# A three-layer fp32 forward pass on one core: step order changed at eleven places of the program

## Chip, core and metric

One NeuronCore of a Trainium2 chip runs the whole program in one launch. The metric is the device time of that core in microseconds (us); lower is better.

## What is computed

Batch 1, 256 tokens, width 1024, all in fp32. Three layers follow each other, and each ends in a feed-forward net with 2816 hidden channels:

```python
# layer 1: three branches of one projection, gated and summed, then w_out
y_a = mla_branch(u_mla, ...) @ w_br_mla       # softmax attention, 8 heads, low-rank q and kv, rope
y_b = fox_branch(u_fox, ...) @ w_br_fox       # softmax attention with a decay, 8 heads
y_c = ssm_branch(u_ssm, ...) @ w_br_ssm       # state-space scan, 16 heads, gated by z, normalised
merged = g[:, :, 0] * y_a + g[:, :, 1] * y_b + g[:, :, 2] * y_c
x = x + merged @ w_out
x = x + conv_ffn(rms_norm(x, norm_ffn_g), ffn_w_up, ffn_conv_w, ffn_conv_b, ffn_w_down)
# layer 2: causal mean pools and attention over 256 memory tokens, w_out, SwiGLU
# layer 3: stick-breaking attention (12 heads, keys and values from kv_norm(x) @ w_kv),
#          attention over the memory tokens (4 heads), w_out, SwiGLU
A[t, s] = sigmoid(z[t, s]) * prod(1 - sigmoid(z[t, j]) for j in range(s + 1, t))   # s < t
return rmsnorm(x, final_norm)
```

## The kernel before

**Layout.** Activations stay in SBUF with features on the partitions, as tiles [128, chunk, 256 tokens]; `x` is the residual stream with 8 chunks. Weights stream from HBM through a ring of four 1 MB slots (`ring`), one slot for 256 output columns.

**Products in three parts.** A dense group is 256 output columns. Its weights are split into a high part `w_hi` on ACT (line 1498, two halves) and the rest `w_lo` on DVE (line 1938, two halves); the activations are split too (`xhl`, `ssm_h`/`ssm_l`, `xn2h`/`xn2l`). TensorE (PE) sums high x high, high x low and low x high: 48 matmuls of 128x256 a group (line 949), or in the feed-forward layers 16 pairs of one matmul of 512 columns and one of 256 (lines 960, 961). There are two buffers of `w_hi`/`w_lo`, so the split of a group starts only when the group two before it has been multiplied. `split_before` and `SPLIT_AT` say at which group's step the split is issued; on ACT and DVE `splits(g)` stands ahead of the evacuation of group g. Groups go round four PSUM banks.

**Order.** `order()` writes one list `STEPS`, and each engine walks it and issues its own part of each step. `("g", stage, i)` is a dense group; `("half", stage, i)` issues only its first output half, and only on PE: ACT and DVE do nothing at it. The attention heads go in ticks (`ticks`, `first_layer`). At tick t: A, the scores of the pair (t, t+1) on PE; D, the product with the values of the pair before; C, the second PE step of head t-1 (transposes for softmax heads, suffix sums at lines 1358 to 1360 for stick-breaking heads, then DVE line 2298); B, the exponentials of head t (for a stick-breaking head four ACT operations of 128x384, lines 1722 to 1725, then DVE lines 2257, 2258); P, the division by the row sum; E, ACT line 1760; last comes what `fill(t)` gives, the dense groups of that tick. For the third layer the table `more` says which. There are three score banks (`stick_bank`: S0, S1 and T), so the scores of pair h, h+1 wait for DVE line 2298 of head h-2, and D waits for the E of both its heads.

**Output groups of the third layer.** `outb` takes no split: its four groups multiply raw fp32 weights with `mix_sb`, 16 matmuls each (lines 1009, 1043). `("ahead", i, m, k0)` issues a part of outb group i in an earlier tick: chunks 0 to 3 of output half m at k0 = 0 and chunks 4, 5 at k0 = 4; the group's own step then does chunks 6, 7.

**Norms.** `late(name, groups)` puts a norm behind the four quarters of a projection. For quarter i: DVE adds the group to `x` (line 2137), ACT writes the high part (line 1619), DVE the low part (line 2160), ACT the squares (line 1659), DVE adds them (line 2181). The first group of the next stage is multiplied in the order of the quarters, without the row factor; `total_sums` on PE (`"ns"`) follows, then Ln and Exp on ACT (lines 1681, 1690) give `rstd`, and DVE multiplies it in when it evacuates. Where the last group of a projection frees the buffer that the next split needs (`LAST_PAIR`), that split comes behind the squares of quarter 3: line 1668 on ACT, `behind` on DVE. Two small norms m6 and m7 of the first layer (keys of the MLA heads) stand in ticks 0 and 1 of the fox heads.

**Feed-forward nets.** `ffn(name)`: 22 up groups, each followed on ACT and DVE by the split for the group two later. In net "1" DVE scales the bank (line 2332) and does four convolution taps (line 2352), ACT applies SiLU (line 1818), and GpSimd (POOL) makes the hidden product and its two parts (lines 2502, 2504, 2506) for j = 0 to 19; for j = 20 and 21 DVE does these three (lines 2365, 2368, 2370).

**Ends.** PE begins with 11 matmuls of ones (line 1404) before the first weights are there. At the end DVE multiplies the four quarters of `x` with `rstd` (line 2210) and SyncE (SP) sends each to HBM (line 903).

Of the kernel before, what the change touches and what calls it, by code (L numbers as in the profile page):

```python
# [23 lines left out]
ALU = mybir.AluOpType  # L24
# [6 lines left out]
P = 128  # L31
# [227 lines left out]
def order():  # L259
# [69 lines left out]
    def first_layer(heads):  # L329
# [5 lines left out]
        for t in range(n + 2):  # L335
# [14 lines left out]
            out += {0: [("nm", "m6"), ("sq", "m7")], 1: [("nm", "m7")]}.get(t, [])  # L350
# [19 lines left out]
    st += [("g", "brs", 0), ("ns", "ssm", 3), ("nm", "ssm")] + [("g", "brs", n) for n in range(1, 4)]  # L370
# [155 lines left out]
def build(nc, cst_at, par_at, x_in, mem_in, pos_in, cst_in, cst2_in, par_in, w, out):  # L526
    with ExitStack() as ctx:
# [169 lines left out]
        tapped = sem("tapped")  # L697
        scaled, rest_copied = sem("scaled"), sem("rest_copied")
# [130 lines left out]
        def _(sp):  # L829
# [78 lines left out]
        def _(pe):  # L908
# [158 lines left out]
            def group(stage, i, half=None):  # L1067
# [81 lines left out]
                elif stage == "brs":  # L1149
                    last = feature3(stage, i, 256, two3, after("ssm") if i == 0 else None, (ssm_h, ssm_l))  # L1150
# [252 lines left out]
            for _ in range(11):  # L1403
# [69 lines left out]
        def _(act):  # L1473
# [18 lines left out]
            def high(raw, q, wait_landed, wait_used=None):  # L1492
# [4 lines left out]
                for a, e in halves_of(raw.shape[-1]):  # L1497
# [8 lines left out]
            def splits(g, behind=None):  # L1506
                for key in split_at(g, behind):
                    u, q = LOAD[key], SPLITS[key]
                    if q == 0:
                        continue  # L1510
                    high(ring[:, u % RING, 0:w[key[0]].shape[-1]], q, (landed[u % RING], 16 * (u // RING + 1)),
                         used(BY_SPLIT[q - 2]) if q >= 2 else None)
# [108 lines left out]

            def squares(name, i=None):
# [290 lines left out]
        def _(dve):  # L1913
# [20 lines left out]
            def low(raw, q, it, count):  # L1934

                for m, (a, e) in enumerate(halves_of(raw.shape[-1])):
                    dve.wait_ge(hi_ready, it * 2 * RING + (2 * count - 1 + m))
# [3 lines left out]
                last.then_inc(lo_ready, 1)  # L1941
# [605 lines left out]
```

## Time and profile before

| | |
|---|---|
| median of 3 runs | 1108.15 us (1107.95 to 1108.33) |
| the profiled execution | 1107.72 us; its span, first to last instruction: 1105.9 us |
| mean granted TensorE clock | 0.997 |
| busy | PE 98%, PE weight loads 89%, DVE 74%, ACT 57%, POOL 9% |
| PE instructions | 7444 matmul records |
| HBM traffic | 190.97 MB, 173 GB/s |

Busy time is the union of an engine's instructions from their start to their modelled end. Matmuls are pipelined: those of 256 columns start 0.118 us apart and each is shown for 0.28 us, so a wait appears some 0.17 us shorter than what it costs. The 16 matmuls of an outb group are recorded as 32 entries that start 0.2165 us apart; the scores of a pair of stick-breaking heads occupy PE for 0.85 us and the C of one for 0.89.

### The profile page before, as it was taken

How to read it: one execution, taken by the hardware profiler on the slowest of the kernel's cores; microseconds unless marked ns; L12 is line 12 of the kernel's file. 1: busy time of each engine (PE TensorE's matmuls, PEld its weight loads, DVE VectorE, ACT ScalarE, POOL GpSimd, SP SyncE). 2: the span in 40 equal slices, each digit the busy share in tenths (PEclk: the TensorE clock that was granted, in tenths of full speed). 3: DMA queues.
4: the chain of work that ended last, by engine and by line, in shares of the span. 5: the costliest groups of instructions: out<-in, count | busy, mean ns of one | idle time of the engine just before them, and what ended most of it. 6: DMA issues, size and time to landing. Idle time of an engine off the chain costs nothing.

```text
span 1105.9 us, 19448 instructions
## 1 busy us (share of the span) xinstructions
PE 1080.5 (98%) x7444; PEld 980.5 (89%) x7444; DVE 815.1 (74%) x1332; ACT 632.8 (57%) x1046; POOL 98.7 (9%) x112
## 2 busy tenths in 40 slices
PE   8999999999999999999999999999999999999997
PEld 8986999999999999988979888888899778888886
DVE  6856898668777999956765888876756447888654
ACT  6675767556657666644335655545567545555453
POOL 0000211056200333300000000000000000000000
PEclk9999999999999999999999999999999999999999
DMA  9345533455545556456426555445643036554451
GB/s 355 142 165 187 209 136 107 173 192 198 183 161 190 177 180 233 154 182 221 162 77 228 177 191 191 165 158 183 233 149 136 17 117 231 188 191 166 166 189 47
DMA packets 33899, 190.97 MB, mean 173 GB/s; under 512 B 3916, under 2 KB 7268, under 8 KB 16676
## 3 DMA queue, kind: packets, MB, share of 16 engines
q1 hardware_dynamic: 33252, 188.95, 48.4%
q10 hardware_dynamic: 576, 1.05, 0.3%
q8 instruction: 48, 0.79, 0.3%
q14 instruction: 23, 0.19, 0.0%
HBM read 187.86 MB, written 2.12 MB: 172 GB/s over the span
## 4 chain that ended last, share of the span: by engine, by line
PE 70%; DVE 16%; ACT 7%; issue 5%; DMA 1%; DVEq 1%; SPq 0%; ACTq 0%
PE bank L949 26%; PE bank L960 14%; PE bank L961 7%; DVE w_lo L1938 7%; DVE acc L2352 3%; PE S L960 3%; PE bank L1009 3%; ACT w_hi L1498 2%; PE O L960 2%; PE T L960 2%; PE S L961 2%; PE bank L1018 1%; PE O L1394 1%; PE O L961 1%; DVE pr L2332 1%
## 5 line engine op out<-in xcount | busy, mean ns | idle before, releaser
L1938 DVE TENSOR_TENSOR w_lo<-ring,w_hi 128x1024 fp32r<-128x1024 f32 (+2 forms) x354 | 379.3, 1113 | 97.9 <-ACT w_hi L1498 96.7
L1498 ACT ACTIVATE w_hi<-ring 128x1024 fp32r<-128x1024 f32 (+2 forms) x354 | 322.6, 961 | 192.7 <-PE bank L949 125.2
L949 PE MATMUL bank<-xhl,w_hi 128*128 128x256 f32 x1792 | 321.0, 282 | 1.9 <-DVE w_lo L1938 1.5
L949 PEld LDWEIGHTS bank<-xhl,w_hi 128*128 128x128 f32 x1792 | 273.4, 188 | 6.3 <-issue 4.9
L949 PE MATMUL bank<-xhl,w_lo 128*128 128x256 f32 x896 | 250.3, 279 | 0.0
L960 PE MATMUL bank<-hid,w_hi 128*128 128x512 f32 x528 | 184.9, 394 | 3.3 <-DVE w_lo L1938 2.9
L949 PEld LDWEIGHTS bank<-xhl,w_lo 128*128 128x128 f32 x896 | 168.8, 188 | 0.0
L961 PE MATMUL bank<-hid,w_lo 128*128 128x256 f32 x528 | 147.8, 280 | 0.0
L960 PE MATMUL bank<-xhl,w_hi 128*128 128x512 f32 x352 | 124.9, 392 | 1.3 <-DVE w_lo L1938 1.2
L960 PEld LDWEIGHTS bank<-hid,w_hi 128*128 128x128 f32 x528 | 99.2, 188 | 28.5 <-issue 6.0
L961 PE MATMUL bank<-xhl,w_lo 128*128 128x256 f32 x352 | 99.3, 282 | 0.0
L961 PEld LDWEIGHTS bank<-hid,w_lo 128*128 128x128 f32 x528 | 99.2, 188 | 0.0
L960 PEld LDWEIGHTS bank<-xhl,w_hi 128*128 128x128 f32 x352 | 66.1, 188 | 15.7 <-DVE w_lo L1938 2.0
L1793 ACT ACTIVATE pr<-bank 128x256 f32<-128x256 f32 x44 | 16.9, 385 | 106.4 <-PE S L961 52.2
L961 PEld LDWEIGHTS bank<-xhl,w_lo 128*128 128x128 f32 x352 | 66.7, 190 | 0.1
L2352 DVE SCALAR_TENSOR_TENSOR acc<-pr,par,acc 128x255 f32<-128x255 f32 (+1 forms) x88 | 56.4, 680 | 3.0 <-DVE acc L2352 0.2
L960 PE MATMUL S<-xhl,w_hi 128*128 128x512 f32 x160 | 56.3, 390 | 0.0
L961 PE MATMUL S<-xhl,w_lo 128*128 128x256 f32 x160 | 45.2, 282 | 0.0
L1619 ACT ACTIVATE xhl<-x,cst,par 128x256 fp32r<-128x256 f32 x40 | 21.8, 593 | 32.3 <-DVE x L2137 25.1
L2339 DVE TENSOR_TENSOR acc<-bank,pr 128x256 f32<-128x256 f32 x44 | 18.7, 425 | 26.8 <-ACT pr L1793 26.8
L960 PEld LDWEIGHTS S<-xhl,w_hi 128*128 128x128 f32 x160 | 30.0, 188 | 6.2
L960 PE MATMUL T<-xhl,w_hi 128*128 128x512 f32 x96 | 34.1, 390 | 0.0
(354 smaller groups left out, 1941.1 us busy)
## 6 DMA issues: line engine op xcount, KB each, us to landing
ring<-w_up SPq DMA_DIRECT2D x22, 1024.0 KB, 4.8
ring<-w_upa SPq DMA_DIRECT2D x22, 1024.0 KB, 4.8
ring<-w_upb SPq DMA_DIRECT2D x22, 1024.0 KB, 4.8
ring<-w_gate SPq DMA_DIRECT2D x12, 1024.0 KB, 4.9
ring<-w_down SPq DMA_DIRECT2D x16, 704.0 KB, 4.0
ring<-w_downa SPq DMA_DIRECT2D x16, 704.0 KB, 4.1
ring<-w_downb SPq DMA_DIRECT2D x16, 704.0 KB, 4.2
ring<-w_xbc SPq DMA_DIRECT2D x6, 1024.0 KB, 5.0
```

The costliest lines, as they stand in the source:

```text
L949: last = mm(out, lhs, rhs, start=(start and k == 0 and (a, b) == (0, 0)), **kw, stop=(whole and k == ks[-1] and (a, b) == (1, 0)))
L960: mm(both, w_of(0, k), x2_of(k), start=k == 0, stop=False, skip_group_check=True)
L961: last = mm(main, w_of(1, k), x2_of(k)[:, 0, :], start=False, stop=whole and k == ks[-1], skip_group_check=True)
L1009: last = mm(b[p0:p0 + width, m * S:m * S + S], W[0:kp, k * wide + c0:k * wide + c0 + width], src(k), start=(k == 0), stop=(k == kc - 1))
L1018: last = mm(b[:, tt * wide:(tt + 1) * wide], src(k)[:, tt * P:(tt + 1) * P], W[:, k * wide:(k + 1) * wide], start=(k == 0), stop=(k == kc ...
L1394: mm(outs[m][:, 0:S], vs[m][:, 0, :], probs[m][:, 0:S], start=True, stop=False)
L1498: A(w_hi[:, q % 2, a:e], raw[:, a:e], ACT.Copy).then_inc(hi_ready, 1)
L1619: last = A(hi[:, c, :], src[:, c, :], ACT.Identity, bias=C("zero"), scale=Pm(gain, c))
L1793: last = A(pr[:, r, m * S:(m + 1) * S], b[:, S:2 * S], ACT.Copy)
L1938: last = V.tensor_tensor(w_lo[:, q % 2, a:e], raw[:, a:e], w_hi[:, q % 2, a:e], ALU.subtract)
L2339: last = V.tensor_tensor(y[:, m * S:(m + 1) * S], b[:, 0:S], pr[:, r, m * S:(m + 1) * S], ALU.add)
L2352: ins = stt(part, y[:, m * S:(m + 1) * S - late], par[:, bass.ds(j * 8 + o, 1)], part, ALU.mult, ALU.add)
```

## The change

Seven kinds of edit. (1) The norm steps `nm m6`, `sq m7` and `nm m7` stand one tick later. (2) The first half of `brs 1` is issued on PE between `brs 0` and the sums of the norm "ssm". (3) `more` gives the dense groups of the stick-breaking ticks out anew. (4) Three outb groups are begun ahead instead of two, and the first two in one tick each. (5) For "ffn1" and "ffna" the split behind quarter 3 is cut in two: its first half stands ahead of the high and low part of quarter 3, the second where the whole stood. (6) In net "1" the hidden product of j = 20 goes to POOL. (7) PE begins with 17 matmuls of ones; at the end POOL multiplies quarter 2, and the quarters are sent in the order 0, 1, 3, 2.

```diff
@@ order(), first_layer
-            out += {0: [("nm", "m6"), ("sq", "m7")], 1: [("nm", "m7")]}.get(t, [])
+            out += {1: [("nm", "m6"), ("sq", "m7")], 2: [("nm", "m7")]}.get(t, [])
...
-    st += [("g", "brs", 0), ("ns", "ssm", 3), ("nm", "ssm")] + [("g", "brs", n) for n in range(1, 4)]
+    st += [("g", "brs", 0), ("half", "brs", 1), ("ns", "ssm", 3), ("nm", "ssm")] + [("g", "brs", n) for n in range(1, 4)]
...
-    more = [sum(both("kk", 1), []), *both("qq", 1), both("kv", 1)[0], both("kv", 1)[1] + both("kk", 2)[0],
-            both("kk", 2)[1] + both("qq", 2)[0], both("qq", 2)[1], *both("kv", 2), *both("qmb", 0)]
-    more += [[("ahead", i, m, 0)] for i in range(2) for m in range(2)]
-    more += [[("ahead", i, m, 4) for m in range(2)] for i in range(2)] + [[]]
+    more = [sum(both("kk", 1), []), sum(both("qq", 1), []), *both("kv", 1), *both("kk", 2), sum(both("qq", 2), []),
+            *both("kv", 2), *both("qmb", 0)]
+    more += [[("ahead", i, m, 0) for m in range(2)] for i in range(2)] + [[("ahead", 2, m, 0)] for m in range(2)]
+    more += [[("ahead", i, m, 4) for m in range(2)] for i in range(3)]
@@ SyncE
-            for i in range(4):
-                sp.wait_ge(normed, NORMED["last"] + i + 1)
+            for n, i in enumerate((0, 1, 3, 2)):
+                sp.wait_ge(*((pool_normed, 1) if i == 2 else (normed, NORMED["last"] + n + 1)))
@@ TensorE
-            for _ in range(11):
+            for _ in range(17):
@@ ACT, squares(name, i)
                 for wait in input_ready(name, i) if (name, i) != ("last", 3) else ():
                     act.wait_ge(*wait)
+                if name in ("ffn1", "ffna") and i == 3:
+                    split_behind(name, 0)
                 if name in LATE and name not in ("x1", "ssm"):
                     high_parts(name, i, 0)
...
                 if i == 3:
                     n["wide"] += 1
-                    for g, norm in LAST_PAIR.items():
-                        if norm == name:
-                            splits(g, behind=True)
+                    split_behind(name, 1 if name in ("ffn1", "ffna") else None)
@@ DVE, step "sq"
+                    early = s[1] in ("ffn1", "ffna")
+                    if early and s[2] == 3:
+                        behind(s[1], 0)
                     if s[1] not in ("x1", "ssm"):
                         low_parts(*s[1:], 0)
                     add_squares(*s[1:])
                     if s[2] == 3:
-                        behind(s[1])
+                        behind(s[1], 1 if early else None)
@@ DVE, end of ffn("1")
-                    dve.wait_ge(up_hid, NFF // RING * RING)
-                    for j in range(NFF // RING * RING, NFF):
-                        hidden(j, j % RING, j // RING)
+                    dve.wait_ge(hid_t, NFF - 1)
+                    dve.wait_ge(hid_high, NFF - 1)
+                    dve.wait_ge(up_hid, NFF - 1)
+                    hidden(NFF - 1, (NFF - 1) % RING, (NFF - 1) // RING)
@@ GpSimd
+                if s == ("nm", "last"):
+                    pool.wait_ge(gained, 3)
+                    pool.wait_ge(rstd_ready, len(NORM_AT))
+                    Q.tensor_tensor(x[:, 4:6, :], x[:, 4:6, :], rstd[:, 0:S].unsqueeze(1).to_broadcast([P, 2, S]), ALU.mult)\
+                        .then_inc(pool_normed, 1)
...
+                    up(NFF - 2, 0, NFF // RING, base)
```

Three places show what the order of the instructions becomes. In this list x3 is the number of equal instructions, and a line number is that of the kernel it is from.

ACT, third layer, ticks 3 to 5: `v_sb` is the evacuation of kv group 1, the operations on `sc` and `G` are the B of heads 4 and 5, `pT` is an E. Before:

```order
L1722 ACTIVATE sc<-S,cst 128x384
L1723 ACTIVATE sc<-S,cst 128x384
L1724 ACTIVATE sc<-sc,cst 128x384
L1725 ACTIVATE sc<-sc,cst 128x384
L1760 ACTIVATE pT<-pr,cst 128x384
L1498 ACTIVATE w_hi<-ring 128x1024 x2
L1530 ACTIVATE v_sb<-bank,cst,rT 128x256 x2
L1768 ACTIVATE mix_sb<-O 128x256
```

and with the change:

```order
L1501 ACTIVATE w_hi<-ring 128x1024 x2
L1533 ACTIVATE v_sb<-bank,cst,rT 128x256 x2
L1731 ACTIVATE sc<-S,cst 128x384
L1732 ACTIVATE sc<-S,cst 128x384
L1733 ACTIVATE sc<-sc,cst 128x384
L1734 ACTIVATE sc<-sc,cst 128x384
L1769 ACTIVATE pT<-pr,cst 128x384
L1777 ACTIVATE mix_sb<-O 128x256
```

The split and the evacuation that followed B and E of the tick now stand ahead of them; `mix_sb` is the output of the D that waits for this E.

PE, third layer, ticks 11 to 13: L1043 (L1044 with the change) is work of `ahead`, `S<-mk,qm` the scores of memory heads 0, 1, `T<-pr` the C of head 11, `O<-pT,v_sb` the D of heads 10, 11. Before:

```order
L1043 MATMUL bank<-mix_sb,ring 128x256 x4
L1341 MATMUL S<-mk,qm 128x256 x2
L1343 MATMUL S<-mk,qm 128x256 x2
L1358 MATMUL T<-pr,cst 128x256
L1359 MATMUL T<-pr,cst 128x128
L1360 MATMUL T<-pr,cst 128x128
L1043 MATMUL bank<-mix_sb,ring 128x256 x4
L1394 MATMUL O<-pT,v_sb 64x256 x2
```

and with the change:

```order
L1044 MATMUL bank<-mix_sb,ring 128x256 x8
L1342 MATMUL S<-mk,qm 128x256 x2
L1344 MATMUL S<-mk,qm 128x256 x2
L1359 MATMUL T<-pr,cst 128x256
L1360 MATMUL T<-pr,cst 128x128
L1361 MATMUL T<-pr,cst 128x128
L1044 MATMUL bank<-mix_sb,ring 128x256 x8
L1395 MATMUL O<-pT,v_sb 64x256 x2
```

Eight matmuls of 256 columns stand where four did, ahead of the scores and between C and D.

DVE, end of the norm "ffn1" (quarter 3): `x<-bank` adds the last group, `xhl` is the low part, `lnv` adds the squares, `w_lo` is the split of up group 1. Before:

```order
L2137 SCALAR_TENSOR_TENSOR x<-bank,x 128x512
L2160 SCALAR_TENSOR_TENSOR xhl<-x,par,xhl 128x256 x2
L2181 TENSOR_TENSOR lnv<-lnv,sqr 128x512
L1938 TENSOR_TENSOR w_lo<-ring,w_hi 128x1024 x2
L2375 UNCONDITIONAL_BRANCH
```

and with the change:

```order
L2149 SCALAR_TENSOR_TENSOR x<-bank,x 128x512
L1949 TENSOR_TENSOR w_lo<-ring,w_hi 128x1024
L2172 SCALAR_TENSOR_TENSOR xhl<-x,par,xhl 128x256 x2
L2193 TENSOR_TENSOR lnv<-lnv,sqr 128x512
L1949 TENSOR_TENSOR w_lo<-ring,w_hi 128x1024
L2389 UNCONDITIONAL_BRANCH
```

One of the two halves of the split now stands between the addition and the low part of quarter 3.

## Rows read from the trace of the kernel before

**Rows 1.** The page, busy time of the engines.
```profile
PE 1080.5 (98%) x7444; PEld 980.5 (89%) x7444; DVE 815.1 (74%) x1332; ACT 632.8 (57%) x1046; POOL 98.7 (9%) x112
```
**Rows 2.** Waits of PE: us in total, times, longest.
```profile
PE bank L960 <- DVE w_lo L1938: 4.1, 9, 1.2
```
**Rows 3.** Timeline of PE, 109 to 124: start, us, instruction, [idle before <- releaser].
```profile
109.33 0.67 PE L1280 MATMUL S<-sqr,cst 96*128 96x512 f32 x1 [0.73 <-DVE sc L2268]
...
123.97 0.37 PE L949 MATMUL bank<-xhl,w_hi 128*128 128x256 f32 x1
```
**Rows 4.** Timeline of DVE, 124 to 125.
```profile
124.46 0.56 DVE L2268 SCALAR_TENSOR_TENSOR sc<-S,G 128x384 f32<-128x384 f32 x1
```
**Rows 5.** Timeline of PE and DVE, 297 to 309, the norm "ssm".
```profile
297.90 1.13 PE L930 MATMUL T<-lnv,cst 128*128 128x256 f32 x4 [1.08 <-DVE lnv L2181]
...
306.20 2.35 DVE L1938 TENSOR_TENSOR w_lo<-ring,w_hi 128x1024 fp32r<-128x1024 f32 x2
```
**Rows 6.** Timeline of DVE and PE at the end of the norm "ffn1".
```profile
341.73 0.88 DVE L2160 SCALAR_TENSOR_TENSOR xhl<-x,par,xhl 128x256 fp32r<-128x256 f32 x2 [1.16 <-ACT xhl L1619]
...
342.77 0.40 PE L949 MATMUL bank<-xhl,w_hi 128*128 128x256 f32 x2
...
345.71 0.39 PE L949 MATMUL bank<-xhl,w_hi 128*128 128x256 f32 x1 [0.50 <-DVE w_lo L1938]
```
**Rows 7.** Timeline of ACT: the high part of a split of 256 output columns.
```profile
835.58 2.02 ACT L1498 ACTIVATE w_hi<-ring 128x1024 fp32r<-128x1024 f32 x2 [1.39 <-PE bank L949]
```
**Rows 8.** Timeline of PE at the end of the norm "ffna".
```profile
610.91 0.50 PE L960 MATMUL bank<-xhl,w_hi 128*128 128x512 f32 x1 [1.24 <-DVE w_lo L1938]
```
**Rows 9.** Timeline of DVE and PE, 461 to 473, last hidden channels of net "1".
```profile
461.77 2.83 DVE L2352 SCALAR_TENSOR_TENSOR acc<-pr,par,acc 128x255 f32<-128x255 f32 x4
...
466.73 1.78 DVE L2352 SCALAR_TENSOR_TENSOR acc<-pr,par,acc 128x255 f32<-128x255 f32 x4
...
470.67 3.37 DVE L1938 TENSOR_TENSOR w_lo<-ring,w_hi 128x704 fp32r<-128x704 f32 x4
...
472.50 0.47 PE L960 MATMUL bank<-hid,w_hi 128*128 128x512 f32 x1 [1.08 <-DVE w_lo L1938]
```
**Rows 10.** Timeline of ACT, SiLU of j = 21.
```profile
468.54 0.51 ACT L1818 ACTIVATE sg<-acc,cst 128x256 f32<-128x256 f32 x1 [1.81 <-DVE acc L2352]
```
**Rows 11.** Timeline of PE and ACT in the stick-breaking ticks, 820 to 839.
```profile
820.60 0.48 PE L1325 MATMUL T<-qk_sb 64*128 64x256 f32 x1 [0.88 <-DVE pr L2298]
...
831.34 0.58 ACT L1722 ACTIVATE sc<-S,cst 128x384 f32<-128x384 f32 x1 [0.47 <-PE T L1327]
...
837.50 1.00 ACT L1530 ACTIVATE v_sb<-bank,cst,rT 128x256 f32<-128x256 f32 x2
```
**Rows 12.** Timeline of PE, 878 to 894, D of heads 10 and 11, outb 0.
```profile
878.83 0.65 PE L1394 MATMUL O<-pT,v_sb 128*64 128x256 f32 x4 [1.42 <-ACT pT L1760]
...
893.60 0.46 PE L1043 MATMUL bank<-mix_sb,ring 128*128 128x256 f32 x1 [0.60 <-ACT mix_sb L1768]
```
**Rows 13.** Timeline of DVE and PE, quarter 3 of the norm "ffnb".
```profile
911.14 0.69 DVE L2137 SCALAR_TENSOR_TENSOR x<-bank,x 128x512 f32<-128x512 f32 x1 [1.14 <-PE bank L1009]
913.00 0.88 DVE L2160 SCALAR_TENSOR_TENSOR xhl<-x,par,xhl 128x256 fp32r<-128x256 f32 x2 [1.16 <-ACT xhl L1619]
...
915.11 0.39 PE L960 MATMUL bank<-xhl,w_hi 128*128 128x512 f32 x1
```
**Rows 14.** Timeline of DVE, the last multiplications.
```profile
1100.20 2.50 DVE L2210 TENSOR_TENSOR x<-x,rstd 128x512 f32<-128x512 f32 x4 [2.44 <-ACT rstd L1690]
```
**Rows 15.** Timeline of POOL: one operation alone, then beside a split.
```profile
109.74 0.72 POOL L2490 TENSOR_TENSOR G<-merged,cst 128x256 f32<-128x256 f32 x1
...
125.58 1.82 POOL L2490 TENSOR_TENSOR G<-merged,cst 128x256 f32<-128x256 f32 x1
```
**Rows 16.** PE at the start: timeline, and busy us (and clock) by stretch.
```profile
15.43 0.38 PE L949 MATMUL bank<-xrh,w_hi 128*128 128x256 f32 x1 [0.45 <-DVE w_lo L1938]
7.70:11.00 3.30, 3.12 (x15) 2.82 (x14) 2.54 (x6) 3.30 (x8) 0.00 (x0) 0.50 1.06 433
```

More of the change, by code:

```diff
@@ L697, in build @@
         tapped = sem("tapped")
+        pool_normed = sem("pool_normed")
         scaled, rest_copied = sem("scaled"), sem("rest_copied")
@@ L1149, in group @@
                 elif stage == "brs":
-                    last = feature3(stage, i, 256, two3, after("ssm") if i == 0 else None, (ssm_h, ssm_l))
+                    last = feature3(stage, i, 256, two3, after("ssm") if i == 0 else None, (ssm_h, ssm_l), half)
                 elif stage == "out1":
@@ L1490, in got, with high @@
                 return banks[g % RING], evacuated[g % RING]
-            def high(raw, q, wait_landed, wait_used=None):
+            def high(raw, q, wait_landed, wait_used=None, half=None):
                 act.wait_ge(*wait_landed)
@@ L1496, in high @@
                     act.wait_ge(*wait_used)
-                for a, e in halves_of(raw.shape[-1]):
+                for m, (a, e) in enumerate(halves_of(raw.shape[-1])):
+                    if half not in (None, m):
+                        continue
                     A(w_hi[:, q % 2, a:e], raw[:, a:e], ACT.Copy).then_inc(hi_ready, 1)
@@ L1504, in head_high, with splits @@
                 A(w_hi[:, 0, a:e], ring[:, 0, a:e], ACT.Copy).then_inc(hi_ready if i % 2 else head_hi, 1)
-            def splits(g, behind=None):
+            def splits(g, behind=None, half=None):
                 for key in split_at(g, behind):
@@ L1511, in splits @@
                     high(ring[:, u % RING, 0:w[key[0]].shape[-1]], q, (landed[u % RING], 16 * (u // RING + 1)),
-                         used(BY_SPLIT[q - 2]) if q >= 2 else None)
+                         used(BY_SPLIT[q - 2]) if q >= 2 else None, half)
             def group(stage, i):
@@ L1620, in high_parts, with split_behind @@
                 last.then_inc(xh_ready, 1)
+            def split_behind(name, half):
+                for g, norm in LAST_PAIR.items():
+                    if norm == name:
+                        splits(g, True, half)
             def squares(name, i=None):
@@ L1932, in copied, with low @@
                 dve.wait_ge(evacuated[g % RING], g // RING + 1)
-            def low(raw, q, it, count):
+            def low(raw, q, it, count, half=None):
                 for m, (a, e) in enumerate(halves_of(raw.shape[-1])):
+                    if half not in (None, m):
+                        continue
                     dve.wait_ge(hi_ready, it * 2 * RING + (2 * count - 1 + m))
@@ L1940, in low @@
                         last.then_inc(head_low, 1)
-                last.then_inc(lo_ready, 1)
+                if half != 0:
+                    last.then_inc(lo_ready, 1)
             def head_rest(i):
@@ L1948, in head_rest, with splits @@
                     .then_inc(lo_ready if i == 3 else head_low, 1)
-            def splits(g, behind=None):
+            def splits(g, behind=None, half=None):
                 for key in split_at(g, behind):
@@ L1954, in splits @@
                         continue
-                    low(ring[:, u % RING, 0:w[key[0]].shape[-1]], q, 0, q + 1)
+                    low(ring[:, u % RING, 0:w[key[0]].shape[-1]], q, 0, q + 1, half)
             def pair(ap, i):
@@ L2162, in low_parts, with behind @@
                 last.then_inc(normed, 1)
-            def behind(name):
+            def behind(name, half):
                 for g, norm in LAST_PAIR.items():
                     if norm == name:
-                        splits(g, behind=True)
+                        splits(g, True, half)
             def add_squares(name, i):
```

2 lines of the change are left out of this document (added).

## The prediction

> **What bounds the kernel.** I read the busy line of the page first: PE is busy 1080.5 us of a span of 1105.9 [rows 1]. Another engine can matter only where PE waits for it. The waits of PE come next; their largest line is the low part of a weight split, 4.1 us in nine waits [rows 2]. All of them are short, and the change touches eleven or so. Since the matmuls stay (six small ones apart), the question is how many of those waits go and how many new ones the new order makes. So I read the timelines around each edited place, and compare when the result that PE needs would be ready with when PE would ask for it. A wait shown on PE costs some 0.17 more than is shown, because the matmul before it is drawn 0.28 long while the next could have started 0.118 after it. Times are of the profiled execution, 1107.72 us; the median is 0.43 higher, and differences go onto the median. About 0.2% (2.2 us) is what a measurement of this kernel tells from no change.
>
> **m6 and m7 a tick later.** The product for m6 waits 0.73 for the masked scores [rows 3]; with 0.17 and a little of the work behind it, 0.95 goes. In tick 2 the product of m7 then stands on PE right behind the C of fox head 1, where now a dense matmul starts at 123.97 [rows 3]. Its bank is freed by DVE at 124.46 + 0.56 = 125.02 [rows 4]. A wait of 1.05 comes: **+0.1** (bounds: no new wait, -0.95; DVE later by one operation, +0.7).
>
> **Half of brs 1 ahead of the sums.** It removes 1.08 + 0.17 = 1.25 at 297.90 [rows 5]. The half group is 24 x 0.118 = 2.83 of work, so the sums and `rstd` come 2.83 - 1.25 = 1.6 later. DVE's chain from the sums to the split of brs 3 starts 8.30 behind the sums [rows 5]; about 0.55 of that is idle and can go. The split would start at 306.20 + 1.6 - 0.55 = 307.2 and end 2.2 later, at 309.4. PE, 1.25 earlier than now, asks for it at about 308.8. So 0.55 comes back: **-0.7** (bounds -1.25 and 0).
>
> **ffn1 and ffna, the split cut in two.** At ffn1 DVE now writes the low part of quarter 3 at 341.73 to 342.61, PE takes it from 342.77, and after the sums it waits 0.50 for the split [rows 6]. With the change ACT and DVE do one half of the split first. On ACT one of 1024 columns takes half of 2.02 [rows 7], and the low part waits for ACT's high part [rows 6]: it is ready 1.0 later, at 343.65. PE waits 0.95 there. The split is then done earlier, but the sums end 0.95 later too, which eats the 0.67 saved: **+0.3** (bounds: -0.67, if the low part were hidden, and +0.8). At ffna PE waits 1.24 behind the sums [rows 8]. DVE's operations from the last addition to the end of the split are the same ones in another order, and PE's next product needs the last of them: **0.0** (bounds -1.4, if ACT's part was the limit, and +0.8).
>
> **Hidden product j = 20 on POOL.** The four taps take 2.83 while POOL makes a hidden product and 1.78 while it doesn't [rows 9]. Those of j = 21 are the 1.78 ones, and would now run beside POOL: +1.05. DVE saves one hidden product, half of the time from 468.51 to 470.67, 1.08 [rows 9]. But this product now covers ACT's SiLU of j = 21, 0.51 long and started by the last tap [rows 10]; without it DVE stands still for that. Sum 1.05 - 1.08 + 0.51 = **+0.5**, behind a wait of PE that is already 1.08 [rows 9] (bounds: taps undisturbed, -0.55; POOL ready late, +0.9).
>
> **Stick-breaking ticks.** The wait of 0.88 for line 2298 before the scores of heads 2, 3 goes (1.05) [rows 11], and about 0.8 of waits of 0.1 to 0.2 behind it and before the C of heads 3 and 7. Where a split and an evacuation now stand ahead of B and E on ACT, the D that needs this E is later. For kv 1: split 2.02, `v_sb` 1.00, four operations of B at 0.59 each, E 0.6, in all 6.0 behind the end of the group [rows 7, 11]. PE has only the scores (0.85), C (0.89) and half a group (2.83) to do, 4.6, so it waits 1.5 in that tick; the same sum gives 0.8 for kk 2 in the tick of D of heads 0, 1. **+0.5** (bounds: new waits absent, -1.9; both twice as long, +2.8).
>
> **Memory heads, three groups ahead.** D of heads 10, 11 waits 1.42 and outb 0 waits 0.60 [rows 12]; with 0.17 each and 0.3 at C of head 11 some 2.6 goes, of which 0.5 returns as shorter cover. The third group's 12 matmuls, 24 entries of 0.2165, are 5.2 of work moved ahead of outb 0, so its own part starts at 893.60 + 5.2 - 2.1 + 0.5 (the term before) = 897.2. From there the norm "ffnb" is a chain on ACT and DVE: from 893.60 to the low part of quarter 3 at 913.88 are 20.3, with 1.14 and 0.2 of idle that waits for PE [rows 12, 13]. At least 18.9 stay, so the low part is ready at 916.1. PE, with 5.2 less of work in between, would be at it 21.5 - 5.2 = 16.3 behind, at 913.5 [rows 12, 13]: a new wait of 2.6. Now it is there at 915.11, so both third-layer parts together give **+1.0**, of which this one has +0.5. The 5.2 us of matmuls moved ahead fill waits, and the chain behind them gives the time back (bounds: chain no limit, -2.1; +1.5 with its idle unchanged).
>
> **Ends.** The four last multiplications take 2.50, 0.62 each [rows 14]. With POOL on quarter 2, DVE is done 0.6 earlier. POOL's operation of 256 columns took 0.72 alone, and 1.82 beside a split [rows 15]; one of 512 is then between 1.3 and 3.2. It starts with quarter 0, and its transfer goes last. At 1.3 the last transfer leaves 0.6 earlier, at 3.2 it leaves 0.7 later: **+0.1**. The row of 1.82 is longer by about one DVE operation of the split. The Trainium skill (SBUF — State Buffer, "Who interferes with whom") says that a DVE instruction with two SBUF inputs contends with a GpSimd instruction that reads SBUF, and that the loser fully blocks. By that rule three DVE operations and POOL's stand in a row here, and this term is +0.7 instead of +0.1. The row agrees with the rule. The warm-up of 17 ones instead of 11 lies ahead of weights that come no sooner: the first full group waits for DVE's split at 15.43, whatever the clock was before [rows 16]: **0.0**.
>
> **Sum:** 0.1 - 0.7 + 0.3 + 0.0 + 0.5 + 0.5 + 0.5 + 0.1 + 0.0 = +1.3. That gives 1109.0 for an execution like the profiled one and **1109.5** on the median.
>
> **Rivals.** (a) All eleven waits go and none comes. They are 0.95, 1.25, 0.67, 1.4 (ffna), 1.25 (hidden product), 1.05 + 0.8, 2.6 and 0.6 at the end, in all 10.6, which gives 1097.6. For it: PE has no more work. Against it: four of them end on DVE and ACT chains that lose no operation. (b) The new waits are real but half as long. They are 1.05, 0.55, 0.95, 0.5 + 1.25 (hidden), 1.5 + 0.8 and 2.6, in all 9.2; half is 4.6, and 1109.5 - 4.6 gives 1104.9. This happens if ACT and DVE stand further ahead in the new order than my sums of rows let them. (c) **Slower, by the clock at the start.** Between 7.7 and 11.0 the granted clock was 0.50, that is 1.2 GHz, with 15 matmuls in 3.12 us, 0.208 each [rows 16]. Ahead of that PE had stood idle between the ones and the weights. If the longer warm-up shifts that stretch so that some 25 more matmuls of the first group run at the low level, 25 x (0.208 - 0.118) = 2.3 comes on top: 1111.8. It decides from the point where PE's first group is later than the split at 15.43. The Trainium skill (TensorE: Matmul & The Clock Gate, Part 1) says the gate goes by how busy PE has been recently; which side of it the six more ones fall no row of before shows. (d) **Slower, by ACT in the ticks.** If the splits that now stand ahead of B and E start later than the end of the group they wait for, the new waits of D are twice as long: 2.8 instead of 0.5 for the ticks, 1111.8. (e) The new order only renames what PE waits for: each wait that is removed comes back at the next step with its size, as at m7, where -0.95 meets +1.05. Then nothing changes: 1108.15.
>
> **Chances.** Forecast 0.50, with a range of its own of 1106 to 1111 (same 0.42, faster 0.03, slower 0.05); (a) 0.07; (b) 0.24, of it same 0.04; (c) 0.08; (d) 0.06; (e) 0.05. So faster 0.30, same 0.51, slower 0.19. The range leaves out (a), the lower part of (b) and a part of (c): 1103.8 to 1111.6.
>
> **What would show it.** Waits of PE shown at the product of m7 (about 0.9 for `sc`), at the low part of quarter 3 in ffn1 (0.8), at D of heads 0, 1 and 2, 3 (0.6 and 1.3 for `pT`) and in up group 0 of net "b" (2.4 for `xhl`) would prove the steps; the waits of 1.42 and 0.88 gone in any case. If the sum of PE's waits falls by over 4 us, the chains are shorter than I take them, and the forecast is wrong on the fast side; a stretch at clock 0.50 that reaches beyond 15.4 would prove (c).

## Result: 1113.21 us where 1109.5 was forecast, and the profile after

| | before | changed |
|---|---|---|
| median of 5 runs, us | 1108.15 | 1113.21 |
| lowest to highest | 1107.95 to 1108.33 | 1111.45 to 1115.08 |
| ratio | | 1.0043, 95% interval 1.0029 to 1.0058 |
| the profiled execution | 1107.72 | 1111.45 |
| mean granted TensorE clock of single executions | 0.997 (the profiled one) | 0.994 to 0.998 |

The change makes the kernel slower by 0.4%. Two things are to be explained. The profiled execution, one of the quickest of the changed kernel, is already 3.7 us above that of before. The five of it spread over 3.6 us, where the five of before agree within 0.4. (In the later batches, of 21 to 33 executions, before spreads by 1.2 to 2.4 itself, so some of that contrast is due to five being few.) The page of the changed kernel, busy line:

```profile
PE 1081.8 (97%) x7456; PEld 981.1 (88%) x7456; DVE 814.2 (73%) x1328; ACT 636.0 (57%) x1048; POOL 104.3 (9%) x116
```

Against [rows 1] PE has 12 records more (six ones) and 1.3 us more of busy time; ACT has 3.2 us more in two instructions more. Those two instructions are loads of function tables, 1.28 each; they are the first surprise, below. The waits of PE in the changed kernel (us, times, longest):

```profile
PE bank L961 <- DVE xhl L2172: 3.2, 2, 2.3
PE bank L961 <- DVE w_lo L1949: 3.1, 8, 1.1
PE T L1368 <- DVE pr L2303: 2.4, 3, 1.1
...
PE O L1395 <- ACT pT L1769: 1.1, 1, 1.1
...
PE S L1281 <- DVE sc L2282: 1.0, 1, 1.0
PE bank L950 <- DVE xhl L2172: 0.8, 1, 0.8
PE bank L961 <- DVE hid L2384: 0.6, 1, 0.6
```

The largest line of before, `w_lo` [rows 2], went from 4.1 to 3.1. In its place stand waits that before did not have: for the low part of a quarter (3.2 and 0.8), for the masked scores before the product of m7 (1.0, where before had 0.7 at the product for m6), and for a hidden product (0.6). Placed over each other, matmul by matmul, the two traces show the same work later by these amounts: +0.4 behind m7's product, +1.2 behind the C near 145, +0.7 behind `brs 3`, +1.0 behind ffn1, +1.7 at the last hidden product, +1.8 behind ffna, +2.35 at quarter 3 of ffnb, +2.75 at the last matmul, +3.7 at the end of the span. The largest steps are at places that I had priced at 0.1: m6/m7 and the end. The stops themselves, in time order (timeline of PE, changed kernel):

```profile
344.51 0.50 PE L950 MATMUL bank<-xhl,w_hi 128*128 128x256 f32 x2 [0.79 <-DVE xhl L2172]
...
610.53 0.50 PE L961 MATMUL bank<-xhl,w_hi 128*128 128x512 f32 x1 [0.94 <-DVE xhl L2172]
...
829.64 0.65 PE L1395 MATMUL O<-pT,v_sb 128*64 128x256 f32 x4 [0.56 <-issue]
...
840.36 0.65 PE L1395 MATMUL O<-pT,v_sb 128*64 128x256 f32 x4 [1.12 <-ACT pT L1769]
...
917.45 0.50 PE L961 MATMUL bank<-xhl,w_hi 128*128 128x512 f32 x1 [2.31 <-DVE xhl L2172]
```

Four of them are the stops that the prediction placed: 0.8 at ffn1, 0.6 and 1.3 at the two D, 2.4 at ffnb. For the D at 829.64 the profile names no releaser (`issue`), so that it waits for `pT` is not shown there. The fifth, 0.94 at 610.53 in ffna, stands ahead of the sums, where the prediction had no new wait; it takes the place of the 1.24 behind them [rows 8]. The start of the kernel does not matter: between 7.7 and 11.0 the granted clock was 0.50 in the profile of before [rows 16] and 1.00 in that of the changed kernel, and PE's wait for the split ends at 15.43 and at 15.40.

### The profile page after: what moved, and what is told of

Its sections match the earlier page's. It is cut to its first block, busy times and chain, and to the rows that moved or that the text cites. A ratio compares the mean times of both kernels' runs of the same rounds, so it can differ in the third digit from the quotient of the medians.

```text
span 1109.7 us, 19481 instructions
## 1 busy us (share of the span) xinstructions
PE 1081.8 (97%) x7456; PEld 981.1 (88%) x7456; DVE 814.2 (73%) x1328; ACT 636.0 (57%) x1048; POOL 104.3 (9%) x116
## 3 DMA queue, kind: packets, MB, share of 16 engines
HBM read 187.86 MB, written 2.12 MB: 171 GB/s over the span
## 4 chain that ended last, share of the span: by engine, by line
PE 69%; DVE 17%; ACT 7%; issue 6%; DVEq 1%; DMA 1%; SPq 0%; ACTq 0%
PE bank L950 26%; PE bank L961 14%; DVE w_lo L1949 7%; PE bank L962 7%; DVE acc L2366 4%; PE S L961 3%; ACT w_hi L1501 2%; PE O L961 2%; PE S L962 2%; PE T L961 2%; PE bank L1010 2%; PE bank L1044 1%; PE bank L1019 1%; PE O L1395 1%; PE O L962 1%
```

## The experiments

Sixteen kernels were run beside before, whose median in the four batches was 1108.10, 1108.07, 1107.98 and 1108.00, with 1.2, 1.4, 1.4 and 2.4 from its lowest to its highest. Kernels with one edit had 11 executions, the larger ones mostly 5. "Before plus one edit" is the kernel before with that part of the change's diff alone.

### The 17 ones, the end, the cut split

The first question was where the spread of 3.6 us comes from. Rival (c) had it at the start.

Before plus the 17 ones:
```diff
-            for _ in range(11):
+            for _ in range(17):
```


> The kernel before with 17 ones at the start instead of 11 and nothing else. Theory 1: the spread of the changed kernel (1111.45 to 1115.08, where before lies within 0.4) comes from the start, where in some executions the half clock lasts longer. Then this kernel spreads by some us too, with a median of 1109 to 1111, and an execution at the top shows 0.50 behind 15.4 us. Theory 2: the spread comes from the new order or from POOL at the end. Then this kernel gives 1108.15 within 0.3, and its executions agree within 0.5.

Measured: 1108.08 (1107.64 to 1108.52), ratio 0.9999 (0.9990 to 1.0008). The warm-up costs and gives nothing.

The changed kernel with 11 ones:
```diff
-            for _ in range(17):
+            for _ in range(11):
```


> The changed kernel with 11 ones again. Theory 1: its executions agree within 0.5 and the median is that of the undisturbed profiled execution, 1111.5. Theory 2: median 1113.2 and a spread of 3 us as with 17 ones.

Measured: 1111.91 (1111.51 to 1114.94), ratio 1.0043 (1.0029 to 1.0056). The spread of 3.4 stays. The slowest two executions had a mean clock of 0.993 and 0.995, the three quick ones 0.998. So a longer time goes with a lower mean clock, and 11 ones do not cure it: six ones more at the start are not the cause.

The same with the old end as well:
```diff
-                        if i == 2:
-                            continue
...
-            for n, i in enumerate((0, 1, 3, 2)):
-                sp.wait_ge(*((pool_normed, 1) if i == 2 else (normed, NORMED["last"] + n + 1)))
+            for i in range(4):
+                sp.wait_ge(normed, NORMED["last"] + i + 1)
```


> The changed kernel with 11 ones and with the old end (DVE multiplies all four quarters, sent 0, 1, 2, 3). The two profiles give the end 1.0 us, of it 0.46 on DVE: so 1.0 less than the kernel with 11 ones alone, 1110.5. If POOL at the end did not cost anything and the 1.0 were chance, both are the same within 0.3. If the spread comes from POOL at the end, it is gone here and not there.

Measured: 1112.31 (1111.19 to 1113.19), ratio 1.0038 (1.0025 to 1.0052). Inconclusive: a step of 1.0 can't be seen in five executions that spread by 2 to 3. A spread of 2.0 is left with the old end, so the end alone does not make it.

Before plus the split cut in two for ffn1 and ffna (in ACT and DVE):
```diff
+                    early = s[1] in ("ffn1", "ffna")
+                    if early and s[2] == 3:
+                        behind(s[1], 0)
                     if s[1] not in ("x1", "ssm"):
                         low_parts(*s[1:], 0)
                     add_squares(*s[1:])
                     if s[2] == 3:
-                        behind(s[1])
+                        behind(s[1], 1 if early else None)
```


> The kernel before with only the split behind quarter 3 cut in two, for ffn1 and ffna. Read from the changed kernel's trace: +0.3 at ffn1 and +0.1 at ffna, so 1108.5. My prediction had +0.3 and 0.0. A rival: the wait for the low part of quarter 3 costs in full, +1.0 and +1.2, 1110.4.

Measured: 1108.53 (1108.10 to 1108.89), ratio 1.0004 (0.9995 to 1.0013), +0.43. As forecast within 0.1: a wait behind the sums is exchanged for one ahead of them.

### The third layer and net 1, alone

Before plus the new ticks (`more`, first statement of the diff), before plus the three groups ahead (its last two), and both:

> The kernel before with only the new dense groups of the stick-breaking ticks; outb groups ahead as before. In the changed kernel's undisturbed trace this stretch gives +0.4: 1108.5. Theory A: the spread of the changed kernel (up to 3.6 above its lowest, at a mean clock of 0.994 instead of 0.998) comes from new stops of PE in these ticks, behind which the clock falls in some executions; then this kernel spreads by 2 us or more, median above 1109. Theory B: the spread comes from the memory heads and the norm ffnb; then it agrees within 1 us.

> The kernel before with only the three outb groups ahead. Undisturbed: +0.1 (my prediction +0.5), 1108.2 to 1108.6. Theory B: its executions spread by 2 us or more and the clock of some is 0.993 to 0.995, since the matmuls that stood before ffnb are gone and PE now stops for 2.3 there; median above 1109. Theory A: within 1 us.

> Both third-layer parts on the kernel before. Undisturbed +0.5: 1108.6, and with the spread, wherever in the third layer it arises, a median of 1109.5 to 1110.5. If neither this kernel nor the two others spreads, the cause is in the first layer or in net 1.

Measured: ticks 1108.31 (1108.10 to 1109.00), +0.24, ratio 1.0003 (0.9993 to 1.0012). Ahead 1109.66 (1108.26 to 1110.49), +1.59, ratio 1.0012 (1.0002 to 1.0021). Both 1109.58 (1108.31 to 1110.38), +1.51, ratio 1.0013 (1.0004 to 1.0022). Theory A falls and theory B stands: the ticks are harmless within what eleven executions tell. With three groups ahead seven of eleven executions lie at 1109.41 and above, and the four others between 1108.26 and 1108.84; the mean clock of the seven is 0.995 to 0.997, that of the four 0.998. The profiled execution of this kernel is one of the seven. Timeline of PE, first the stop, then what follows it:

```profile
912.77 0.28 PE L961 MATMUL T<-xhl,w_lo 128*128 128x256 f32 x1
915.36 0.50 PE L960 MATMUL bank<-xhl,w_hi 128*128 128x512 f32 x1 [2.31 <-DVE xhl L2160]
...
915.81 0.39 PE L960 MATMUL bank<-xhl,w_hi 128*128 128x512 f32 x1
...
916.16 0.39 PE L960 MATMUL T<-xhl,w_hi 128*128 128x512 f32 x1
...
918.52 0.63 PE L960 MATMUL bank<-xhl,w_hi 128*128 128x512 f32 x1
918.95 0.41 PE L961 MATMUL bank<-xhl,w_lo 128*128 128x256 f32 x1
919.16 0.63 PE L960 MATMUL bank<-xhl,w_hi 128*128 128x512 f32 x1
```

and the same trace by stretches (busy us of PE, PEld, DVE, ACT, POOL, each with its count; then granted clock, DMA share, GB/s):

```profile
912.80:915.30 2.50, 0.25 (x2) 0.00 (x0) 1.34 (x4) 1.70 (x3) 0.00 (x0) 1.00 1.01 413
915.30:916.50 1.20, 1.14 (x6) 1.01 (x7) 1.03 (x3) 0.00 (x0) 0.00 (x0) 1.00 0.84 335
916.50:918.20 1.70, 1.70 (x7) 1.42 (x6) 0.00 (x0) 0.08 (x1) 0.00 (x0) 0.54 0.95 381
918.20:920.00 1.80, 1.80 (x7) 1.51 (x7) 0.13 (x1) 1.71 (x5) 0.00 (x0) 0.50 0.16 68
```

In the profiled execution of the changed kernel, which has the same stop of 2.31 (ending at 917.45), the stretch as far behind it reads:

```profile
918.60:920.30 1.70, 1.70 (x11) 1.50 (x10) 0.00 (x0) 0.62 (x2) 0.00 (x0) 1.00 1.00 419
```

In the kernel with three groups ahead PE stands still for 2.31. The next matmuls run at full clock, and one microsecond later the granted clock is 0.54, that is the 1.2 GHz level for nearly the whole stretch, and 0.50 up to 920.0. Seven matmuls fall into 1.70 us there, eleven in the changed kernel, where the clock stayed at 1.00. A pair of a 512- and a 256-column matmul starts every 0.35 at first (915.81, 916.16) and every 0.64 then (918.52, 919.16). The lag behind the trace of before grows here from 0.25 to 1.94. Half speed from about 916.6 to 920.0 loses just that 1.7. So the stop costs about 0.3 where the clock holds and 1.7 more in this execution, where it falls. That the clock of the other six fell at the same place is inferred from their times: this is the only kept trace with a low clock in the middle of the program. The Trainium skill (TensorE: Matmul & The Clock Gate, Part 1) has the gate set by how busy PE has been recently; the trace agrees, with the clock at 1.00 during the stop and 0.54 after it.

Before plus the hidden product of j = 20 on POOL:
```diff
-                    dve.wait_ge(up_hid, NFF // RING * RING)
-                    for j in range(NFF // RING * RING, NFF):
-                        hidden(j, j % RING, j // RING)
+                    dve.wait_ge(up_hid, NFF - 1)
+                    hidden(NFF - 1, (NFF - 1) % RING, (NFF - 1) // RING)
...
+                    up(NFF - 2, 0, NFF // RING, base)
```


> The kernel before with the hidden product of j = 20 on POOL. The changed kernel's trace has +0.75 here, my prediction +0.5: 1108.9. A rival: POOL and DVE only swap the work and nothing is paid, 1108.15; or the product is the one at which the spread arises, above 1109.5.

Measured: 1108.89 (1108.46 to 1110.68), ratio 1.0010 (1.0001 to 1.0020), +0.82. Four of eleven are at 1109.88 and above, 1.4 or more over the lowest: perhaps a second place at which the clock falls. The profiled execution was not one of them, and before spreads by 1.4 in this batch itself, so this is read from a few times alone and is not shown. The timeline of DVE and then of PE in this kernel:

```profile
467.10 2.77 DVE L2352 SCALAR_TENSOR_TENSOR acc<-pr,par,acc 128x255 f32<-128x255 f32 x4
470.54 0.42 DVE L2365 TENSOR_TENSOR sg<-sg,acc 128x256 f32<-128x256 f32 x1 [0.68 <-ACT sg L1818]
...
471.67 3.36 DVE L1938 TENSOR_TENSOR w_lo<-ring,w_hi 128x704 fp32r<-128x704 f32 x4
```
```profile
471.81 0.50 PE L960 MATMUL bank<-hid,w_hi 128*128 128x512 f32 x1 [0.58 <-DVE hid L2370]
472.14 0.28 PE L961 MATMUL bank<-hid,w_lo 128*128 128x256 f32 x1
473.50 0.47 PE L960 MATMUL bank<-hid,w_hi 128*128 128x512 f32 x1 [1.08 <-DVE w_lo L1938]
```

The taps take 2.77 where they took 1.78 [rows 9], DVE then waits 0.68 for SiLU, and the split starts at 471.67 instead of 470.67. Of that 1.0, 0.37 was there already when the four taps began (467.10 instead of 466.73); from there to the split are 4.57 instead of 3.94, +0.63. Each of my three terms is in the rows. What I had not counted is that PE also needs this hidden product itself, 0.58 at 471.81, ahead of the wait for the split that keeps its 1.08. Two stops now stand within 2 us. At the second PE is later than in before by 1.0, of which 0.4 is older: the product's own price is 0.6, as forecast within 0.1, and the rest of the +0.82 is not explained by this trace.

### Filling the stops

If the stop makes the clock fall, work without a purpose in its place should cure it, in spite of being more work. Before plus three groups ahead, with nine matmuls of ones at quarter 3 of ffnb:
```diff
                     for k0 in range(0, KC, step):
+                        if name == "b" and step == 2 and k0 == 6:
+                            idle_ones(9)
```


> The kernel with three outb groups ahead and nothing else, plus nine matmuls of ones (about 2.0 us) issued on PE into a bank that nobody reads at the point where it stood still 2.3 before quarter 3 of ffnb. Theory (clock): the half clock that the last trace shows behind this stop, 916.5 to 919, comes from the stop; with the ones it does not come, all executions lie at 1108.3 within 0.4 and the clock at 0.998. Rival (order): the spread comes from something else in the new order, and the ones change nothing or cost their 2.0: median 1109.7 or more, spread 2.

Measured: 1108.38 (1107.88 to 1108.88), ratio 1.0003 (0.9994 to 1.0013). No execution is above 1108.88, where without the ones seven of eleven were at 1109.41 and above. Two limits: the kernels with the ones ran in later batches than those without, never side by side (before spreads no less in the later ones); and two of the eleven here have a mean clock of 0.995 at 1108.66 and 1108.88, so the mean over a whole execution does not tell where it was low. Its PE timeline (nine matmuls of ones are 18 entries):

```profile
912.71 2.17 PE L915 MATMUL O<-pT 128*128 128x128 f32 x18
915.19 0.50 PE L965 MATMUL bank<-xhl,w_hi 128*128 128x512 f32 x1 [0.30 <-DVE xhl L2167]
```

PE resumes at 915.19, as late as without the ones, and the wait shown is 0.30 instead of 2.31. The chain that sets this moment is DVE's.

The changed kernel with the ones at ffnb and three and five ones around the last hidden products of net 1:
```diff
+                    def hidden(k):
+                        if stage == "down1" and k == 21:
+                            idle_ones(3)
+                        return up_hid, base + k + 1
                     for half in range(2):
+                        if (stage, i, half) == ("down1", 1, 0):
+                            idle_ones(5)
```


> The changed kernel with the nine ones at ffnb and with three and five ones at the two stops of PE around the last hidden products of net 1. Theory (clock): median 1111.5, the changed kernel's lowest, and a spread under 1. If only one of the two places falls, a spread of 1.6 stays. Rival: 1113.2 and a spread of 3.6 as before.

Measured: 1111.73 (1111.41 to 1112.18), ratio 1.0035 (1.0022 to 1.0049). The spread falls from 3.6 to 0.8, less than the 1.6 that was expected if one place still fell. That fits falls at both places, but both were filled at once, in five executions, and no trace shows a fall in net 1: which of the two the ones cured is open. What remains, +3.75 on before, is the price of the new order. Against its own before the changed kernel had +5.06, so about 1.3 more is ascribed to the falls of the clock. This depends on the draw: with 11 ones instead of 17, which cost nothing, the median of five was only 3.8 above before. Of those ten executions five lie between 1111.45 and 1111.91, three are 1.7 to 2.2 above the middle of these, with mean clocks of 0.995 and 0.996, and two are 3.4 and 3.6 above it, with 0.993 and 0.994. Falls of 1.7 at one and at two places would give this.

### The moved norms and brs

Before plus m6 and m7 a tick later (the diff's first edit):

> The kernel before with only m6 and m7 a tick later. The changed kernel's trace gives +0.4 at the product of m7 and +0.8 more at the C of a fox head near 145, together +1.2: 1109.3. My prediction was +0.1: 1108.2.

Measured: 1109.24 (1108.84 to 1109.90), ratio 1.0012 (1.0003 to 1.0021), +1.26. The timeline of ACT and then of DVE in this kernel:

```profile
128.21 1.28 ACT L1681 ACT_TABLE_LOAD   x1
129.51 0.69 ACT L1681 ACTIVATE lnv<-S,cst 128x512 f32<-128x512 f32 x1
130.27 1.28 ACT L1690 ACT_TABLE_LOAD   x1
131.57 0.72 ACT L1690 ACTIVATE rstd<-lnv,cst 128x512 f32<-128x512 f32 x1
```
```profile
132.32 0.74 DVE L2195 SCALAR_TENSOR_TENSOR mqk<-mqk,par,rstd 64x512 f32<-64x512 f32 x1 [3.13 <-ACT rstd L1690]
```

In the kernel before, ACT had this order, and later, at 146, PE had no wait:

```profile
120.19 0.68 ACT L1681 ACTIVATE lnv<-S,cst 128x512 f32<-128x512 f32 x1
120.96 0.72 ACT L1690 ACTIVATE rstd<-lnv,cst 128x512 f32<-128x512 f32 x1
...
125.00 1.28 ACT L1576 ACT_TABLE_LOAD   x1
126.30 0.72 ACT L1576 ACTIVATE sg<-acc,cst 128x512 f32<-128x512 f32 x1
```

and with the norms moved PE has it:

```profile
146.06 0.33 PE L1367 MATMUL T<-cst,pr 128*128 128x128 f32 x1 [0.56 <-DVE pr L2289]
```

In tick 2 the convolution's SiLU (`sg`) has brought another function table onto ACT. The Ln and the Exp of m7 stood ahead of it and needed no load; now each needs one, 1.28 us. DVE stands still for 3.13 until `rstd` is there, 2.56 of it for the two loads, and its splits and the masked scores behind that are late until 146, where PE waits for a division by the row sum. The lag of PE behind the trace of before grows by 0.4 up to the product of m7, which is ahead of the loads, and by 0.8 from there to 146. At other norms the kernel itself asks for one table that holds both functions (`exp_and_ln`, six loads in all, and none at their Ln and Exp); nothing asks for it here, and no kernel was run in which it did. The Trainium skill (ScalarE: Activation LUTs, "What ACT_TABLE_LOAD costs") gives 1.28 for the load, which the rows show, and 1.38 more for a drain, which they don't: Ln starts 1.30 after its load does.

To see whether it is m7's place or m6's own move, before plus m7 alone in tick 2:
```diff
-            out += {0: [("nm", "m6"), ("sq", "m7")], 1: [("nm", "m7")]}.get(t, [])
+            out += {0: [("nm", "m6"), ("sq", "m7")], 2: [("nm", "m7")]}.get(t, [])
```


> The kernel before with only the norm of m7 in tick 2; m6 and the squares of m7 stay in tick 0, so the stop of 0.73 before m6 stays. Theory (table): the cost of the moved norms is that ACT has the table of the SiLU loaded in tick 2 and loads one for Ln and one for Exp, 1.28 each, while DVE waits 3.1 for rstd; then it is +1.2 plus the 0.95 that m6 no longer gives back, 1110.1. Rival (m6): the cost comes from m6 and its squares in tick 1; then it is +0.2 at most, 1108.2.

Measured: 1110.12 (1109.86 to 1111.06), ratio 1.0020 (1.0011 to 1.0029), +2.12. The theory had +2.15. Moving m6 gives 0.9 back, as my prediction said; m7's place costs 2.1. This tells m7 from m6; that the cost of m7's place is the two loads rests on the rows above.

Before plus the half group of brs 1 ahead of the sums:

> The kernel before with only the half group of brs 1 ahead of the sums. My prediction: -0.7, 1107.4. The changed kernel's trace: -0.5, 1107.6. Rival: the row factor comes later than PE wants it by the whole 1.25, 1108.1.

Measured: 1107.65 (1107.19 to 1108.65), -0.33, ratio 0.9998 (0.9989 to 1.0007): its interval holds no change, but the profile shows the parts. Of the 1.25, 0.78 comes back in PE's wait for the split of brs 3, as the prediction had it with 0.55:

```profile
309.94 0.35 PE L949 MATMUL bank<-ssm_h,w_hi 128*128 128x256 f32 x1 [0.61 <-DVE w_lo L1938]
```

### The end alone, the sum, and a better version

Before plus the new end:

> The kernel before with only the new end (POOL multiplies quarter 2, quarters sent 0, 1, 3, 2). My prediction: +0.1, with both ends of the bounds at -0.6 and +0.7. The changed kernel's profile against that of before has DVE's last multiplication 0.46 later and the last transfers 0.6 later still: +1.0, 1109.1. Without contention POOL would be done before DVE and the time falls: 1107.5.

Measured: 1108.99 (1108.55 to 1109.23), +0.99, ratio 1.0006 (0.9997 to 1.0015). DVE and POOL in this kernel:

```profile
1100.38 2.96 DVE L2213 TENSOR_TENSOR x<-x,rstd 128x512 f32<-128x512 f32 x3 [2.44 <-ACT rstd L1691]
```
```profile
1100.49 1.70 POOL L2515 TENSOR_TENSOR x<-x,rstd 128x512 f32<-128x512 f32 x1 [636.08 <-ACT rstd L1691]
```

Three multiplications take 2.96 where four took 2.50 [rows 14]. At 0.62 each they would be 1.9, so DVE loses 1.1 while POOL works for 1.70. The end is at 1103.34, 2.96 behind the first multiplication instead of 2.50: 0.46. Two transfers instead of one are then still to be sent, since quarter 2 goes last: from DVE's end to the span's end are 3.77 (1103.34 to 1107.11) instead of 3.24 (1102.70 to 1105.94), another 0.53. Together 0.99. POOL is done with quarter 2 at 1102.19, ahead of DVE's last; sending it before quarter 3 might save part of the 0.53, which was not tried.

What is left when m6/m7, the cut splits, the hidden product and the end are undone, with the nine ones at ffnb:

> What is left of the change without m6/m7, the cut splits, the hidden product and the end, and with the nine ones at ffnb: brs -0.4, ticks +0.2, three groups ahead +0.3, 17 ones 0: 1108.1. If the parts hinder each other, it is off by more than 0.4.

Measured: 1108.27 (1108.05 to 1109.13), ratio 1.0002 (0.9993 to 1.0011), +0.27. The same parts measured alone add up to -0.33 + 0.24 + 0.40 - 0.02 = +0.29.

The last kernel tries to take the chain at ffnb away instead of covering it. It has the half of brs 1 and the three groups ahead, and the split of up group 1 stands behind quarter 3 instead of in front of it:
```diff
+MOVED = [("upb", 1)]
+for _g in list(SPLIT_AT):
+    SPLIT_AT[_g] = [key for key in SPLIT_AT[_g] if key not in MOVED]
+SPLIT_AT.setdefault(GROUP["outb", 3], []).extend(MOVED)
...
-    late = [key for key in SPLIT_AT.get(g, []) if LAST[BY_SPLIT[SPLITS[key] - 2]] == g
-            and BY_SPLIT[SPLITS[key] - 2] not in HALVES] if g in LAST_PAIR else []
+    late = [key for key in SPLIT_AT.get(g, []) if key in MOVED or (LAST[BY_SPLIT[SPLITS[key] - 2]] == g
+            and BY_SPLIT[SPLITS[key] - 2] not in HALVES)] if g in LAST_PAIR else []
```


> A version meant to be better than both: the kernel before with the half group of brs 1, with three outb groups ahead, and with the split of up group 1 of net b moved from outb 2 to behind quarter 3 of ffnb, so that the low part of quarter 3 is ready 2.3 earlier. The stop of 2.3 at quarter 3 then goes and one of 1.5 to 2 comes before up group 1: -0.4 (brs) and -0.3 against three groups ahead, 1107.6 at the lowest. If the stop of up group 1 is long enough for the clock to fall, the executions spread up to 1109.

Measured: 1106.86 (1106.14 to 1107.32), ratio 0.9988 (0.9979 to 0.9997): 1.1 better than before and the only kernel of the study whose interval lies below 1. Its timeline, DVE and then PE:

```profile
911.32 0.88 DVE L2166 SCALAR_TENSOR_TENSOR xhl<-x,par,xhl 128x256 fp32r<-128x256 f32 x2 [1.16 <-ACT xhl L1625]
...
913.18 2.35 DVE L1944 TENSOR_TENSOR w_lo<-ring,w_hi 128x1024 fp32r<-128x1024 f32 x2
```
```profile
912.25 0.51 PE L966 MATMUL bank<-xhl,w_hi 128*128 128x512 f32 x1
...
915.59 0.50 PE L966 MATMUL bank<-xhl,w_hi 128*128 128x512 f32 x1 [1.24 <-DVE w_lo L1944]
```

PE takes quarter 3 at 912.25 with no stop to speak of (915.36 with the split in front) and then waits 1.24 once, behind the sums, where there was no wait. None of the eleven executions shows a mean clock below 0.996, and they agree within 1.2. Of the 1.6 by which its profiled execution is ahead of that of before, 0.7 is there before the third layer (the half of brs 1, and what executions differ by) and 0.7 comes at ffnb. The moved split without three groups ahead was not run, so how much of that is due to which is open.

## Why the prediction was wrong

The measured terms beside those of the sum (medians against the median of before in the same batch; the intervals of brs, split, ticks and end hold no change, but the terms add up to the whole):

| term | predicted | measured alone |
|---|---|---|
| m6 and m7 | +0.1 | +1.26 |
| half of brs 1 | -0.7 | -0.33 |
| ffn1 and ffna | +0.3 and 0.0 | +0.43 |
| hidden product | +0.5 | +0.82, of which 0.6 is in the trace |
| ticks | +0.5 | +0.24 |
| three groups ahead | +0.5 | +0.40 with the stop filled, +1.59 without |
| end | +0.1 | +0.99 |
| 17 ones | 0.0 | -0.02 |
| sum | +1.3 | +3.8 with the stop at ffnb filled; the whole change with both places filled +3.75 |
| the whole change as it is | +1.3 | +5.06 |

**The step that failed first is the term of m6 and m7.** I followed PE's bank and DVE's masked scores: 0.95 goes and a stop of about 1 comes. That much is there, at +0.4 in the trace instead of +0.1. I did not price what the moved step issues on ACT. Its Ln and Exp land behind a SiLU and need two table loads of 1.28 each, which makes the other 0.8 of the +1.26. It was knowable: in the trace of before the load for the SiLU stands at 125.00, behind the Exp of m7 at 120.96 and in the tick to which m7 moves.

**The second is the end.** Both bounds, -0.6 and +0.7, were too low. I took +0.1 although the row of POOL beside a split [rows 15] and the rule named beside it both pointed to +0.7; and I left out that by sending quarter 2 last, one more transfer waits for DVE's end. The Trainium skill's rule (SBUF — State Buffer, "Who interferes with whom") came nearer than my choice: DVE loses 1.1 beside POOL's 1.70. The four operations did not stand wholly in a row, though: for that the prediction had 3.2, and DVE was done after 2.96.

**The third is the missing cost of a stop.** Quarter 3 of ffnb has the stop that I predicted (2.4 to be shown, 2.31 measured), and its clean price, +0.40, is what I wrote down within 0.1. But a stop in the middle of the program can cost clock after it has ended: 1.7 in the one trace that has it. I had the clock only as rival (c) at the start, which did not happen; falls behind the new stops, seen once at ffnb and supposed at net 1, are what is left to carry the other 1.3 us of the median and most of the spread. This is no step of the sum that was mis-sized but a cost that it did not have.

**Smaller slips of the working.** At ffn1 the row times give 343.65 - 342.77 = 0.88 for the wait, not 0.95, and in the ticks 6.0 - 4.6 is 1.4, not 1.5. Neither changes the forecast by more than 0.1.

**What held.** The stops at ffn1, at both D and at ffnb are where and about as long as forecast, as is the return of brs's gain at brs 3 and the zero of the warm-up. The ticks and three groups ahead were, within the noise, as cheap as forecast or cheaper. Rivals (a), (b), (d) and (e) did not happen. Eleven waits of about 11 us in all were addressed, and more than that came back: the chains on DVE and ACT behind them lost nothing, and two of them, at m7 and at the end, became longer. Only the half of brs 1 gave a part of its wait to keep.

## What to carry to other kernels

Before moving a step, list everything it issues on every engine, with the activation tables that its new neighbours leave behind. Putting one wait in the place of another gained nothing here (+0.43 for the cut splits), and gathering idle time into one stop of 2.3 us made TensorE's clock fall behind it in the trace of one execution. Where PE's work is moved ahead, shorten the chain that ends last as well (here by moving one split behind the quarter that PE needs first). Time each edit alone before they are put together: here the half of brs 1 alone lowered the median, by 0.3 and within the noise, and it took a further change at ffnb to gain 1.1.

## What was not expected of the hardware

The clock falls after a stop, not in it: granted 1.00 from 912.8 to 916.5, 0.54 from 916.5 to 918.2 and 0.50 up to 920.0, behind a stop of 2.31. The same stop in the profiled execution of the changed kernel left it at 1.00. By their times, seven of eleven executions of the same program had the fall. With useless matmuls in the stop none of eleven was that slow, with the end of the stop unmoved. Ln and Exp behind a SiLU each load a table of their own, 1.28 us twice. A 128x512 product of POOL took 1.70, and DVE lost 1.1 beside it.
